# Expert stage: TensorE's gate and up products of the next expert ahead of the transposes and the down product of this one

## What is computed

```python
def hier_moe(x, wg, bg, we, be, w_gate, w_up, w_down):
...
    def expert_block(args):
        xb, e = args
        hdn = jax.nn.silu(xb @ w_gate[e]) * (xb @ w_up[e])
        return hdn @ w_down[e]
...
for l in range(DEPTH):
...
    x = x + mixed @ w_out[l]
    x = x + hier_moe(rmsnorm(x, norm2_g[l]), ...)
return rmsnorm(x, final_g)
```

## Time and profile before

| | us |
|---|---|
| median of 3 runs | 2196.29 (2191.21 to 2240.14) |
| the profiled execution's own time | 2196.54 |
| its span, first to last instruction | 2194.80 |
| expert stage, layer 1: first gate product (L702) to last down product of the overflow block (L717) | 539.04 to 1075.6 |
| expert stage, layer 2: the same | 1613.29 to 2151.5 |
| TensorE busy, share of the span | 1775.6, 81% |
| bytes moved over the span | 240 GB/s in the mean, about 411 to 417 in the expert stages |

### The profile page before, as it was taken

The page is one execution under the profiler, slowest core; times in us unless marked ns, Lnnn a source line. Parts: engine busy times, 40 slices in busy tenths (PEclk is TensorE's granted clock), DMA queues, the critical chain, the costliest instruction groups (busy, mean ns, idle before and its releaser), DMA issues. The chain is left out here.

```text
span 2194.8 us, 24263 instructions
## 1 busy us (share of the span) xinstructions
PE 1775.6 (81%) x9856; PEld 1056.3 (48%) x9856; DVE 588.1 (27%) x1169; ACT 323.2 (15%) x661; POOL 111.7 (5%) x133
## 2 busy tenths in 40 slices
PE   6799999997877867877379999998898777777761
PEld 3346677544544434444134566775554344444430
DVE  1162365533111111111124433565411111111113
ACT  1211233301000000000013123332100000000001
POOL 0010000001000000000100101000010000000001
PEclk9899999898999989989689999999999989998986
DMA  8911100026999999999441211002279999999993
GB/s 284 270 59 52 64 1 1 0 87 243 411 413 414 413 412 412 414 413 399 183 186 41 77 39 39 1 1 87 115 279 410 413 417 411 414 415 412 413 362 129
DMA packets 107428, 527.00 MB, mean 240 GB/s; under 512 B 35044, under 2 KB 35812, under 8 KB 88420
## 3 DMA queue, kind: packets, MB, share of 16 engines
q1 hardware_dynamic: 64740, 476.08, 53.6%
q0 software_dynamic: 38400, 33.79, 4.7%
q10 hardware_dynamic: 4224, 16.25, 3.1%
HBM read 481.83 MB, written 44.04 MB: 240 GB/s over the span
## 5 line engine op out<-in xcount | busy, mean ns | idle before, releaser
L702 PE MATMUL banks<-RING,TOK 128*64 128x256 f32 x4224 | 484.2, 385 | 82.5 <-DMA RING<-in_w_up 41.6
L702 PEld LDWEIGHTS banks<-RING,TOK 128*64 128x64 f32 x4224 | 320.9, 139 | 263.5 <-DMA RING<-in_w_up 56.5
L717 PE MATMUL banks<-RING,XS 128*64 128x512 f32 x1056 | 272.0, 661 | 42.7 <-issue 24.2
L438 PE MATMUL banks<-RING,XNT 128*128 128x512 f32 x512 | 224.1, 593 | 0.0
L717 PEld LDWEIGHTS banks<-RING,XS 128*64 128x64 f32 x1056 | 89.5, 153 | 185.5 <-issue 184.0
L930 ACT ACTIVATE XS<-banks 128x256 f32<-128x256 f32 x64 | 24.5, 383 | 990.3 <-PE banks L702 990.3
L1298 DVE TENSOR_TENSOR XS<-XS,banks 128x256 f32<-128x256 f32 x66 | 27.8, 421 | 505.3 <-PE banks L702 505.3
L438 PEld LDWEIGHTS banks<-RING,XNT 128*128 128x128 f32 x512 | 95.8, 190 | 113.1 <-issue 112.4
L695 PE MATMUL banks<-CF,TOK 128*128 128x128 f32 (+1 forms) x272 | 50.9, 346 | 111.3 <-DMA TOK<-x_slots 109.1
L429 PE MATMUL banks<-XNT,RING 128*128 128x512 f32 x256 | 110.4, 593 | 1.1 <-ACT XNT L787 1.1
L1319 DVE COPY XS<-banks 128x512 f32<-128x512 f32 x64 | 44.3, 691 | 250.0 <-PE banks L717 250.0
(11 more groups left out here) (249 smaller groups left out, 1735.1 us busy)
## 6 DMA issues: line engine op xcount, KB each, us to landing
RING<-in_w_gate SPq DMA_DIRECT2D x66, 2048.0 KB, 27.6
RING<-in_w_up SPq DMA_DIRECT2D x66, 2048.0 KB, 28.1
RING<-in_w_down SPq DMA_DIRECT2D x66, 2048.0 KB, 25.2
RING<-in_w_in_blocks SPq DMA_DIRECT2D x12, 2048.0 KB, 11.3
TOK<-x_slots SPq DMA_DIRECT2D x32, 512.0 KB, 23.8
y_slots<-XS POOLq DMA_DIRECT2D x64, 256.0 KB, 19.4
x_slots<-TOK ACTq DMA_DIRECT2D x11, 1024.0 KB, 32.7
RING<-in_w_out_blocks SPq DMA_DIRECT2D x4, 2048.0 KB, 7.7
```

Of the source, the lines that this page charges most:

```text
L438: last = mm(bank[:, :], XNT[:, k, i * P:(i + 1) * P], w[:, k, :], start=(k == 0), stop=(k == KD - 1))
L702: last = mm(bank[f * CAP:(f + 1) * CAP, 0:256], XT[:, k, h * CAP:(h + 1) * CAP], w[:, k, f * 256:(f + 1) * 256], start=(k == 0), stop=(k = ...
L717: last = mm(PS[5][n * CAP:(n + 1) * CAP, :], HT[:, j, f * CAP:(f + 1) * CAP], w[:, k, n * BN:(n + 1) * BN], start=(k == 0), stop=(k == KF ...
```

## The change

TensorE's program is written one expert deeper: gate and up of expert e+1 stand ahead of the transpose and the down product of expert e. The rows of the next pair are still transposed right after the odd expert's up product, which now puts them ahead of the even expert's transpose and down product. ScalarE's Silu of expert e now waits for `hidden` of expert e-1 (one `HS`), TensorE's gate product waits for `gated` and its up product for `hidden` of the expert before. On VectorE the copy of the rows comes first, then the copy of `HT`, then the multiplication for the next expert, then the copy of y. SP's and GpSimd's programs are the same as before, operation for operation and wait for wait.

```diff
@@ -726,18 +726,27 @@
                         pe.wait_ge(slot_full[slot], 16 * (i + full0[slot] + 1))
                         return SLOT[slot]
 
-                    def expert(i, h, last=False):
+                    def gate_up(i, h, first=False):
 
                         e = 2 * i + h
                         if h == 0:
                             pe.wait_ge(xt_copied, i + 1)
+                        if not first:
+                            pe.wait_ge(gated, e)
                         gate_or_up(weights(0, i, h), PS[2], h).then_inc(gate_ps, 1)
+                        if not first:
+                            pe.wait_ge(hidden, e)
                         gate_or_up(weights(1, i, h), PS[3], h).then_inc(up_ps, 1)
-                        if h == 1 and not last:
-                            pe.wait_ge(rows_full, 16 * (i + 2))
-                            pe.sem_inc(pe_passed, 1)
-                            turn_rows(P, xt_ps)
+
+                    def rows_of(i):
+                        pe.wait_ge(rows_full, 16 * (i + 1))
+                        pe.sem_inc(pe_passed, 1)
+                        turn_rows(P, xt_ps)
+
+                    def hidden_down(i, h):
+                        e = 2 * i + h
                         pe.wait_ge(hidden, e + 1)
+                        pe.sem_inc(pe_passed, 1)
                         turn_hidden(ht_ps)
                         pe.wait_ge(y2_copied, e + 1)
                         pe.wait_ge(ht_copied, e + 1)
@@ -746,11 +755,16 @@
                     pe.wait_ge(route_in, 1)
                     pe.wait_ge(rows_full, 16)
                     turn_rows(P, xt_ps)
+                    gate_up(0, 0, first=True)
                     with pe.Fori(0, NE // 2 - 1) as i:
-                        for h in range(2):
-                            expert(i, h)
-                    expert(NE // 2 - 1, 0)
-                    expert(NE // 2 - 1, 1, last=True)
+                        gate_up(i, 1)
+                        rows_of(i + 1)
+                        hidden_down(i, 0)
+                        gate_up(i + 1, 0)
+                        hidden_down(i, 1)
+                    gate_up(NE // 2 - 1, 1)
+                    hidden_down(NE // 2 - 1, 0)
+                    hidden_down(NE // 2 - 1, 1)
                     nov = pe.value_load(OVI[0:1, NOV:NOV + 1], min_val=0, max_val=NOV)
                     with pe.If(nov > 0):
                         pe.wait_ge(y2_copied, NE + 1)
@@ -923,11 +937,17 @@
                     act.wait_ge(exp_in, 2)
                     ac(RW[:, 656:660], RW[:, 656:660], ACT.Exp).then_inc(exp_done, 1)
 
-                    with act.Fori(0, NE // 2) as i:
+                    def gate(e, first=False):
+                        act.wait_ge(gate_ps, e + 1)
+                        if not first:
+                            act.wait_ge(hidden, e)
+                        ac(HS, PS[2][:, 0:256], ACT.Silu).then_inc(gated, 1)
+
+                    gate(0, first=True)
+                    gate(1)
+                    with act.Fori(1, NE // 2) as i:
                         for h in range(2):
-                            e = 2 * i + h
-                            act.wait_ge(gate_ps, e + 1)
-                            ac(HS, PS[2][:, 0:256], ACT.Silu).then_inc(gated, 1)
+                            gate(2 * i + h)
                     nov = act.value_load(OVI[0:1, NOV:NOV + 1], min_val=0, max_val=NOV)
                     with act.If(nov > 0):
                         with act.Fori(0, nov) as j:
@@ -1303,28 +1323,33 @@
                     dve.wait_ge(xt_ps, 1)
                     copy_rows(P, xt_copied)
                     dve.sem_inc(y2_copied, 1)
-                    def expert(i, h, first=False, last=False):
-                        e = 2 * i + h
+                    def hide_expert(e):
                         dve.wait_ge(gated, e + 1)
                         dve.wait_ge(up_ps, e + 1)
                         hide(hidden)
+
+                    def expert(i, h, first=False, last=False):
+                        e = 2 * i + h
+                        if h == 0 and not last:
+                            dve.wait_ge(xt_ps, i + 2)
+                            copy_rows(P, xt_copied)
                         dve.wait_ge(ht_ps, e + 1)
                         copy_hidden(ht_copied)
-                        if h == 1 and not last:
-                            dve.wait_ge(xt_ps, i + 2)
-                            copy_rows(P, xt_copied)
+                        if h == 0 or not last:
+                            hide_expert(e + 1)
                         dve.wait_ge(y2_ps, e + 1)
                         if not first:
                             dve.wait_ge(y2_stored[h], 8 * NE * layer + 16 * i)
                         V.tensor_copy(YS[h], PS[5][:, :]).then_inc(y2_copied, 1)
 
+                    hide_expert(0)
                     for h in range(2):
                         expert(0, h, first=True)
                     with dve.Fori(1, NE // 2 - 1) as i:
                         for h in range(2):
                             expert(i, h)
-                    expert(NE // 2 - 1, 0)
-                    expert(NE // 2 - 1, 1, last=True)
+                    for h in range(2):
+                        expert(NE // 2 - 1, h, last=True)
                     nov = dve.value_load(OVI[0:1, NOV:NOV + 1], min_val=0, max_val=NOV)
                     with dve.If(nov > 0):
                         dve.wait_ge(y2_stored[0], 8 * NE * (layer + 1))
```

## The result

| | us |
|---|---|
| before, the three runs of the first table and one more | 2218.22 median of 4 (2191.21 to 2243.52) |
| changed kernel | 2421.62 median of 4 (2410.38 to 2449.26) |
| ratio, with its 95% interval | 1.099 (1.088 to 1.111) |
| the profiled executions' own times | 2196.54 and 2410.38, +213.8 |
| expert stage of layer 1, first gate product to the overflow block's last down product | 536.5 and 643.5, +107.0 |

What follows compares the result with a forecast made beforehand. The DMA engines were taken to set the expert stages' pace. Pairs +74.1, start -5.0 and end +12 gave 81 us a layer, 162 in two, on 2196.3: 2358 us, 7.4% slower, range 2222 to 2405.

Steps and rivals of the forecast that it cites:

- the gap: Once a pair in the expert stage, SP's queue runs empty and the DMA engines stand for 0.6 us (0 to 1.4).
- What bounds the kernel: In both expert stages the 16 DMA engines set the pace, share 1.01 and 1.02, while TensorE has slack.
- the step of the earlier trace: Before the change, one pair in four took about 4.1 us longer, read as y stores lying on a few engines each.
- The start of a load: A load into an empty queue needs 2.5 us for start and end beside its 5.04 us transfer.
- The chain: From the turn of a pair's rows to SP's next issue of a down load: 8.2 us (7.6 to 9.0).
- The lost lead: The emptied queue levels the engines, so one y store's share counts in each pair: 5.1 us, lower value 4.1.
- A pair: Time of two experts in the stage: 31.95 + 0.6 + 5.1 = 37.65 us, against 33.04 before.
- Start: At the start of the expert stage, the first turn of rows in the loop comes 5.0 us earlier.
- End: From the last turn of rows to the overflow block's gate product, loads asked for later: +12 us (8 to 14).
- the case with a store's share: At the stage's end, expert 31's up weights land at 31 us after the turn instead of 26.1.
- Sum: 74.1 - 5.0 + 12 = 81 us in a layer, 162 in two, giving 2358 us.
- The signs: Turns 36 to 38.5 us apart without the step, 362 GB/s, share near 0.9, down loads under 20 us, one long gate wait.

Runs made afterwards that it cites:

- e3: The kernel before the change with each y store cut into two of 64 partitions, to spread over the DMA engines; 2224.91 us, no ratio on record.
- e7: Changed kernel with SP's loads in TensorE's new order, y stores spread, and separate semaphores for the overflow block's three matrices; 2190.63 us, ratio 0.979.
- e5: Changed kernel with four extra 128x512 products on TensorE ahead of the wait for the next rows; 2369.93 us, one run.
- e2: Changed kernel with each y store cut into two of 64 partitions, to spread over the DMA engines; 2319.32 us, ratio 1.047.
- e1: Changed kernel with SP's loads in TensorE's new order, gate and up of expert e+1 ahead of down of e; 2256.21 us, ratio 1.026.
- e8: The kernel before the change, old orders kept, with y stores spread and separate semaphores for the overflow block's three matrices; 2191.99 us, ratio 0.982.
- e4: Changed kernel with the next rows' transposes and VectorE's copy of them moved behind the even expert's down product, SP's order unchanged; 2268.93 us, ratio 1.016.

## Why the prediction was right in kind and too small

The measured 2421.62 us lies above the range, whose end was 2405. The step that failed is the size of the gap, the time in which the DMA engines stand still once a pair: 0.6 us in the sum, 1.4 at most, and 2.7 by the runs.

**What bounds the kernel: right.** e3 changed only how the stores are cut up, and the pair fell from 33.04 to 32.27; e7 made TensorE quicker by 13 us and no pair got shorter. The reading that narrow stores explain the step of the earlier trace rows is borne out by e3.

**The gap: right in kind, mis-sized, the larger error.** The prediction said 8.2 + 2.5 = 10.7 against 10.1, a gap of 0.6 us (0 to 1.4). In the trace of the changed kernel, in the mean of 12 pairs, the down load is issued 9.4 us after the turn starts and lands 8.9 us after its issue (8.7 to 9.0). So two steps failed:

- *The start of a load, 2.5 us.* It was taken from the quickest load of gate or up (7.5 us). A down load has another shape (rows of 4 KB to gate's 16). Behind other loads it lands about 5.4 us after the one before it, which leaves 3.5 to 3.6 around the transfer: +1.1. That the shape is the reason no run shows.
- *The chain, 8.2 us (7.6 to 9.0).* Its parts came from a trace in which TensorE waits 3.10 us for the rows and the down product takes 4.57. Behind 3.7 to 4.7 us of waiting the same product takes 5.0 to 6.4. e5 shows that it is the clock: kept busy, TensorE makes it in 3.65 in most pairs, and chain and pair fall by 2.4 and 2.2. The prediction had this risk at the end of its range, and priced it at next to nothing: +1.2.

The turn starts 0.1 us behind the rows' landing, and the second of the two loads ahead lands 9.6 us after it, not 10.1. That makes 9.5 + 3.5 - 9.6 = 3.4 us by this account, and 2.7 by e2 less e3 (in e2 the issue comes at 9.3 and the load ahead lands at 9.8, 3.0 by the same account).

**The lost lead: right, mis-sized the other way.** 5.1 us were taken, and 4.1, the step seen, was named as the lower value. It is 4.3 by the changed kernel less e2. That one share counts and not two fits: two would be 10.2. The observed step should have been the value, and the bytes the bound.

**A pair.** 31.95 + 0.6 + 5.1 = 37.65 was said; e3, e2 and the changed kernel make it 32.27 + 2.7 + 4.3 = 39.24 (rounded terms). So the errors partly cancel: the gap was 2.1 too small, the ground 0.3, and the lost lead 0.8 too large. 31.95 was a little low as the ground, since in the quick pairs of before the stores' bytes were only put off. Over 14 pairs: +93.4 us (453.0 to 546.4) where +74.1 was said.

**Start: -5.0 said, -2.5 measured.** The first two rows are the first gate and up products of both experts in one run and the first turn in the loop, beside the earlier trace rows; the third is SP's down load of expert 2:

```profile
536.96 16.80 PE L702 MATMUL banks<-RING,TOK 128*64 128x256 f32 x128 [1.31 <-DVE TOK L1315]
553.69 1.16 PE L695 MATMUL banks<-CF,TOK 128*128 128x128 f32 x8
...
560.23 0.38 SPq L356 DMA_DIRECT2D RING<-in_w_down  x1
```

The 128 matmuls took 16.80 us instead of 14.2, which again is clock: 0.84 was granted from 537 to 554 us, and e1, with 1.00 in its stretch (578.4 to 592.4), needs 13.97 to the same turn, as e2 does. The order of events was as said, and the first pairs no longer ran ahead: 36.5 us to the second turn (553.69 to 590.16), where it had been 24.6.

**End: +12 (8 to 14) said, +16.5 measured.** The rows beside the earlier trace rows:

```profile
1131.90 3.67 PE L702 MATMUL banks<-RING,TOK 128*64 128x256 f32 x32 [1.29 <-DMA RING<-in_w_up]
...
1141.31 0.60 SPq L386 DMA_DIRECT2D TOK<-x_slots  x1
...
1165.77 9.52 PE L702 MATMUL banks<-RING,TOK 128*64 128x256 f32 x64 [18.57 <-DMA RING<-in_w_down]
```

The last up weights were at hand 31.8 us after the turn at 1100.10, as said for the case with a store's share (31); the issue came at 41.2 instead of 39.5. The miss is in what followed: 24.5 us from there to the gate product, where 0.8 + 2.5 + 15.4 = 18.7 was said, up to 21.5 with a store. The block's rows go first and into an empty queue, and two y stores fall into the same stretch. e7, with spread stores and separate semaphores, starts its gate product 9.6 us after that issue.

**Sum.** 93.4 - 2.5 + 16.5 - 0.4 (the overflow block itself) = 107.0 us in layer 1 and 104.1 in layer 2, against 81: 211 of the 214 us. Of the 52 us that the forecast lacked, 41 are the pairs (19.3 in layer 1, 21.3 in layer 2), 8 the two ends, and the rest the starts and what lies outside the stages. The range fell short because the bounds of the chain came from a trace in whose pairs the queue never ran empty, and a longer chain was given 20 us at the top where it took some 33 (28 pairs of 1.2), beside nearly as much again for the start of the loads.

**The signs.** The step every fourth pair is gone, each pair has one long wait for gate weights (3.75 us), the down loads' median is under 20 (16.6), 351 GB/s and a share of 0.88 stand where 362 and 0.9 were said. Only the spacing, 38.3 to 40.0, is past the 36 to 38.5 named. The 0.58 us waits that the new order takes away were worth nothing, as said: e7 against e8.

## What to carry to other kernels

Where one queue refills a ring in a fixed order, a new order of the consumer frees the slots in a new order too, and the loads must follow it, or no product whose slot the queue asks for next may stand behind a wait for that same queue (e1 and e4: either mends it). A queue that never runs empty hides more than the start of its loads: here it also hid narrow stores (e1 and e4), so before it is let run empty, look for narrow transfers and spread them; with the overflow block's waits set apart that was worth about 2% even in the old order (e8). And a chain that was measured beside short waits is not the chain behind long ones: price TensorE's part of it at the lower clock, and take the start of a load from a load of the same shape.

## What was not expected of the hardware

- A 2048 KB load into an empty queue took 7.4 to 7.8 us with 16 KB rows (gate, at the start of the stage) and 8.7 to 9.0 with 4 KB rows (down, in the pairs; 8.6 to 9.2 beside spread stores, in e2), while behind other loads they are only 0.5 us apart (4.9 and 5.4). Why the second needs some 1.1 us more to get going is open.
- With spread stores the stage moves 422 GB/s instead of 413 at nearly the same share (1.01 and 1.02), and the whole kernel has 27648 fewer packets under 512 B (35044 to 7396). That the packets are the cause wasn't tried apart.
- The clock of a mixer differs between the profiled executions. In e1 the window of the mixer ahead of the expert stage has a granted clock of 0.60 and lasts some 33 us longer than in the kernel before, whose row stands second, for the same code:

```profile
360.00:476.00 116.00, 109.71 (x398) 74.04 (x398) 49.01 (x119) 30.31 (x84) 0.00 (x0) 0.60 0.00 1
```
```profile
353.00:436.00 83.00, 76.81 (x405) 53.52 (x404) 48.53 (x119) 30.14 (x85) 0.00 (x0) 0.90 0.00 1
```

The first expert stage began between 537 and 578 us in the ten profiled executions (539.0 before, 537.0 changed, 578.4 in e1, 576.6 in e2). No run tells what decides it, nor whether a kernel keeps to one of these times. It is where the totals of these executions move by 40 us although no code of the mixers differs, and why the stages were compared.
